# Expert weights in 8 KB and 4 KB rows: gate and up weights with channel d at partition d // 8, down weights as two full-width blocks

## What is computed

```python
mod = c_act @ ada_w[l] + ada_b[l]
shift1, scale1, gate1, shift2, scale2, gate2 = jnp.split(mod, 6, axis=-1)
h = rms_norm(x, norm1_g[l]) * (1.0 + scale1) + shift1
x = x + gate1 * hybrid_mixer(h, ...)
h = rms_norm(x, norm2_g[l]) * (1.0 + scale2) + shift2
# grouped_moe: a router picks one of 4 groups of 4 experts for each token, and 2 experts in it
for e in range(16):
    hid = silu(t @ w_gate[e]) * (t @ w_up[e])        # t: 256 x 1024, w_gate, w_up: 1024 x 512
    out = out + combine[:, e:e + 1] * (hid @ w_down[e])   # w_down: 512 x 1024
x = x + gate2 * out
```

## Time and profile before

| | us |
|---|---|
| median of 3 runs | 1594.67 |
| lowest and highest | 1593.94, 1601.77 |
| the profiled execution | 1598.07 |
| its span, first to last instruction | 1596.3 |

### The profile page before, as it was taken

The page is one execution under the profiler, slowest core; times in us unless marked ns, Lnnn a source line. Parts: engine busy times, 40 slices in busy tenths (PEclk is TensorE's granted clock), DMA queues, the critical chain, the costliest instruction groups (busy, mean ns, idle before and its releaser), DMA issues. The chain is left out here.

```text
span 1596.3 us, 18784 instructions
## 1 busy us (share of the span) xinstructions
PE 1418.2 (89%) x7456; PEld 1138.3 (71%) x7456; DVE 1168.3 (73%) x1292; ACT 792.8 (50%) x738; POOL 227.8 (14%) x188
## 2 busy tenths in 40 slices
PE   1887889998689999999988868899985999999998
PEld 1766687786589977766558657777865999776654
DVE  5599358884568878789866963788646665788886
ACT  2465434443353446567655553433434433566674
POOL 2445231110001200000016633111000000000000
PEclk9898999998889999999989989999987999999999
DMA  9634147982078879899965431588704655799994
GB/s 323 201 106 132 53 145 262 309 290 77 17 248 290 306 267 314 299 320 370 340 176 183 131 96 64 193 281 299 255 0 158 213 208 186 266 340 346 355 356 180
DMA packets 175864, 357.44 MB, mean 224 GB/s; under 512 B 13436, under 2 KB 19808, under 8 KB 174752
## 3 DMA queue, kind: packets, MB, share of 16 engines
q1 hardware_dynamic: 163040, 310.99, 56.7%
q0 software_dynamic: 12736, 45.25, 8.1%
HBM read 355.16 MB, written 1.05 MB: 223 GB/s over the span
## 5 line engine op out<-in xcount | busy, mean ns | idle before, releaser
L1517 DVE TENSOR_TENSOR w_low<-ring,w_high_qk_score 128x2048 fp32r<-128x2048 f32 x84 | 192.4, 2291 | 100.7 <-ACT w_high_qk_score L1075 65.5
L604 PE MATMUL bank<-h_high,w_low 128*128 128x256 f32 x864 | 246.2, 285 | 0.0
L1517 DVE TENSOR_TENSOR w_low<-ring,w_high_xbc_sc 128x2048 fp32r<-128x2048 f32 x82 | 187.9, 2291 | 74.2 <-ACT w_high_xbc_sc L1075 44.4
L1517 DVE TENSOR_TENSOR w_low<-ring,w_high_zu 128x2048 fp32r<-128x2048 f32 x82 | 187.7, 2288 | 19.6 <-ACT w_high_zu L1075 10.2
L603 PE MATMUL bank<-w_low,h_high 128*128 128x512 f32 (+2 forms) x480 | 187.2, 390 | 0.0
L1075 ACT ACTIVATE w_high_xbc_sc<-ring 128x2048 fp32r<-128x2048 f32 x64 | 122.8, 1918 | 97.0 <-PE bank L604 97.0
L604 PEld LDWEIGHTS bank<-h_high,w_low 128*128 128x128 f32 x864 | 166.5, 193 | 0.0
L1075 ACT ACTIVATE w_high_qk_score<-ring 128x2048 fp32r<-128x2048 f32 x64 | 122.8, 1918 | 81.2 <-PE bank L604 81.0
L1075 ACT ACTIVATE w_high_zu<-ring 128x2048 fp32r<-128x2048 f32 x64 | 122.4, 1913 | 71.4 <-PE bank L604 71.4
L603 PE MATMUL bank<-w_low,rows_high 128*128 128x512 f32 (+2 forms) x384 | 150.9, 393 | 0.0
L540 POOL TENSOR_TENSOR w_low<-ring,early_high 128x2048 fp32r<-128x2048 f32 (+1 forms) x28 | 125.5, 4494 | 132.5 <-ACT early_high L1083 132.5
(11 more groups left out here) (442 smaller groups left out, 3577.9 us busy)
## 6 DMA issues: line engine op xcount, KB each, us to landing
ring<-in_w_in SPq DMA_DIRECT2D x64, 1024.0 KB, 5.0
ring<-in_exp_w_gate SPq DMA_DIRECT2D x64, 1024.0 KB, 5.5
ring<-in_exp_w_up SPq DMA_DIRECT2D x64, 1024.0 KB, 6.0
ring<-in_exp_w_down SPq DMA_DIRECT2D x64, 1024.0 KB, 5.2
ada_buf<-in_ada_w POOLq DMA_DIRECT2D x40, 512.0 KB, 6.3
PT<-in_ada_w POOLq DMA_DIRECT2D x40, 512.0 KB, 6.8
ring<-in_w_branch SPq DMA_DIRECT2D x12, 1024.0 KB, 5.2
ring<-in_w_out SPq DMA_DIRECT2D x8, 1024.0 KB, 6.6
```

Of the source, the lines that this page charges most:

```text
L604: return mm(out_, ll, rh, start=False, stop=stop, skip_group_check=True)
L1517: V.tensor_tensor(w_low[:, slot, :, cols], ring[:, slot, :, cols], high[:, :, cols], ALU.subtract).then_inc(w_split, 1)
```

## The change

- `w_gate` and `w_up`: channel d is at partition d // 8, block d % 8. A unit (half of the blocks) is then 8 KB in a row for each partition. So that h agrees, the second norm writes `merged` sorted by d % 8 (ACT and DVE read `x_sb` with a step of 8 values), `router_w` is loaded in the same order, the matmuls of `mod67` and `mod89` take every eighth column of `ada_acc`, and `norm2_g` and the two biases of the second norm come in three DMAs of their own on POOL's queue into `cols2` and no longer through `prow` (now 74 rows).
- `w_down`: a unit holds two of the four blocks of 128 FF channels with all 1024 columns, 4 KB in a row. `dense_down` and `rows_down` write both banks from each unit; the last half-sum of a layer waits for the new semaphore `tail_half`.
- `dense_project` and `turn_hidden` are written otherwise but issue the same instructions.

```diff
-for _name, _n in (("norm1", KD), ("norm2", KD), ("adab", 6 * KD), ("scw", SC_K * CT), ("gvg", CT),
+for _name, _n in (("norm1", KD), ("adab", 2 * KD), ("scw", SC_K * CT), ("gvg", CT),
                   ("mcw", M_K * 6), ("mcb", 6), ("mng", CT)):
...
+        cols2 = turns[:, :, :, :].rearrange("p a t f -> p (a t f)")[:, 0:3 * KD].rearrange("p (i k) -> p i k", i=3)
...
-        columns_in = sem("columns_in")
+        columns_in, tail_half = sem("columns_in"), sem("tail_half")
...
-            rows = (("norm1", norm1_g[layer]), ("norm2", norm2_g[layer]), ("adab", ada_b[layer]),
+            rows = (("norm1", norm1_g[layer]), ("adab", ada_b[layer, 0:2 * D_MODEL]),
...
-            wg_v = exp_w_gate.rearrange("l e (k p) n -> (l e) p k n", p=P)
-            wu_v = exp_w_up.rearrange("l e (k p) n -> (l e) p k n", p=P)
+            wg_v = exp_w_gate.rearrange("l e (p k) n -> (l e) p k n", k=KD)
+            wu_v = exp_w_up.rearrange("l e (p k) n -> (l e) p k n", k=KD)
...
-            sp.dma_start(rw[:, :, :], router_w.rearrange("(k p) e -> p k e", p=P)).then_inc(rw_in, 16)
+            sp.dma_start(rw[:, :, :], router_w.rearrange("(p k) e -> p k e", k=KD)).then_inc(rw_in, 16)
...
 
-                def half(n, src):
+                def half(n, src, dst=None):
                     sp.wait_ge(units_read, l * UNITS_L + MOE0 + n + 1)
-                    load(n % RING, src)
+                    load(n % RING, src, dst)
+
+                def down_half(n, expert, j):
+                    half(n, wd_v[expert, :, 2 * j:2 * j + 2, :],
+                         ring[:, n % RING, :, :].rearrange("p (k c) n -> p k (c n)", c=2))
 
...
                     last = this
                 for j in range(2):
-                    half(down_unit(NE - 1) + j, wd_v[last, :, :, j * W:j * W + W])
+                    down_half(down_unit(NE - 1) + j, last, j)
 
             for t in range(TT):
                 sp.wait_ge(x_tile, DEPTH * 4 - 1 + t)
...
+                for i, v in enumerate((ada_b[l, 3 * D_MODEL:4 * D_MODEL], ada_b[l, 4 * D_MODEL:5 * D_MODEL], norm2_g[l])):
+                    pool.dma_start(cols2[:, i, :], v.rearrange("(p k) -> p k", k=KD)).then_inc(gateb_in, 16)
...
                     b = begin("v", name)
-                    for i in range(2):
-                        pe.wait_ge(acc_ready, l * GATE_CHUNKS + n + i + 2)
-                        chunk_columns(b, 4 * i, ada_acc[:, (n + i) % 2, :]).then_inc(acc_used, 1)
+                    assert n % 2 == 0
+                    whole = ada_acc[:, :, :].rearrange("p i n -> p (i n)")
+                    pe.wait_ge(acc_ready, l * GATE_CHUNKS + n + 1 + 2)
+                    for k in range(KD):
+                        last = mm(b[:, k:k + 1], whole[:, k::KD], ones[:, 0:1], start=True, stop=True)
+                        if k >= KD - 2:
+                            last.then_inc(acc_used, 1)
 
...
+                def down_parts(n):
+
+                    return [part.rearrange("p (k c) n -> p k (c n)", c=2) for part in parts(MOE0 + n, n % RING)]
...
                     for j in range(2):
-                        n = down_unit(e) + j
-                        w = parts(MOE0 + n, n % RING)
+                        w = down_parts(down_unit(e) + j)
                         for t in range(TT):
-                            for k in range(CT):
-                                last = exact_mm(bank[:, 4 + 2 * t + j, :],
-                                                [part[:, k, t * P:t * P + P] for part in (hid_high, hid_low)],
-                                                [part[:, k, :] for part in w], k == 0, k == CT - 1)
+                            for c in range(2):
+                                for k in range(2):
+                                    kk = 2 * j + k
+                                    last = exact_mm(bank[:, 4 + 2 * t + c, :],
+                                                    [part[:, kk, t * P:t * P + P] for part in (hid_high, hid_low)],
+                                                    [part[:, k, c * W:c * W + W] for part in w], kk == 0, kk == CT - 1)
                         last.then_inc(units_read, 1)
...
                     for j in range(2):
-                        u = down_unit(e) + j
-                        w = parts(MOE0 + u, u % RING)
-                        for k in range(CT):
-                            last = exact_mm(bank[0:n, 4 + j, :], (hidT_high[:, k, 0:n], hidT_low[:, k, 0:n]),
-                                            [part[:, k, :] for part in w], e % EPG == 0 and k == 0,
-                                            e % EPG == EPG - 1 and k == CT - 1)
+                        w = down_parts(down_unit(e) + j)
+                        for c in range(2):
+                            for k in range(2):
+                                kk = 2 * j + k
+                                last = exact_mm(bank[0:n, 4 + c, :], (hidT_high[:, kk, 0:n], hidT_low[:, kk, 0:n]),
+                                                [part[:, k, c * W:c * W + W] for part in w], e % EPG == 0 and kk == 0,
+                                                e % EPG == EPG - 1 and kk == CT - 1)
+                            if e == NE - 1 and j == 1 and c == 0:
+                                last.then_inc(tail_half, 1)
                         last.then_inc(units_read, 1)
...
+                def sorted_in(t, k0, k1):
+
+                    return x_sb[:, t, :].rearrange("p (q k) -> p k q", k=KD)[:, k0:k1, :]
...
                         if t == norm % 2:
                             act.wait_ge(rstd_ready, done + 1)
-                            A(merged[:, 0, :], x_sb[:, 0, :], ACT.Copy, scale=st[:, 2, 2:3]).then_inc(xn_ready, 1)
+                            if norm == 1:
+                                A(merged[:, 0, :], x_sb[:, 0, :], ACT.Copy, scale=st[:, 2, 2:3]).then_inc(xn_ready, 1)
+                            else:
+                                A(merged[:, 0, :].rearrange("p (k q) -> p k q", k=KD), sorted_in(0, 0, KD), ACT.Copy,
+                                  scale=st[:, 2, 2:3]).then_inc(xn_ready, 1)
                     if norm == 2:
                         act.wait_ge(rstd_ready, done + 2)
-                        A(merged[:, 1, W:], x_sb[:, 1, W:], ACT.Copy, scale=st[:, 2, 3:4]).then_inc(xn_ready, 1)
+                        A(merged[:, 1, W:].rearrange("p (k q) -> p k q", k=HK), sorted_in(1, HK, KD), ACT.Copy,
+                          scale=st[:, 2, 3:4]).then_inc(xn_ready, 1)
...
-                    a0 = (0 if norm == 1 else 3) * KD
-                    step(V.tensor_tensor(modc[:, norm - 1, 1, :], mod_sum[:, norm - 1, 0:KD], col("adab", a0, KD),
-                                         ALU.add))
-                    step(V.tensor_tensor(modc[:, norm - 1, 0, :], mod_sum[:, norm - 1, KD:], col("adab", a0 + KD, KD),
-                                         ALU.add))
+                    shift_b, scale_b, g = ((col("adab", 0, KD), col("adab", KD, KD), col("norm1", 0, KD)) if norm == 1
+                                           else [cols2[:, i, :] for i in range(3)])
+                    step(V.tensor_tensor(modc[:, norm - 1, 1, :], mod_sum[:, norm - 1, 0:KD], shift_b, ALU.add))
+                    step(V.tensor_tensor(modc[:, norm - 1, 0, :], mod_sum[:, norm - 1, KD:], scale_b, ALU.add))
                     settle()
                     V.scalar_tensor_tensor(out=modc[:, norm - 1, 0, :], in0=modc[:, norm - 1, 0, :], scalar=1.0,
-                                           in1=col(f"norm{norm}", 0, KD), op0=ALU.add, op1=ALU.mult
-                                           ).then_inc(modc_ready, 1)
+                                           in1=g, op0=ALU.add, op1=ALU.mult).then_inc(modc_ready, 1)
...
-                dve.wait_ge(gateb_in, (l + 1) * 32)
+                dve.wait_ge(gateb_in, (l + 1) * (5 * 16))
...
-                V.tensor_scalar(merged[:, 1, 0:W], x_sb[:, 1, 0:W], st[:, 2, 3:4], None, ALU.mult).then_inc(xn_ready, 1)
+                V.tensor_scalar(merged[:, 1, 0:W].rearrange("p (k q) -> p k q", k=HK),
+                                x_sb[:, 1, :].rearrange("p (q k) -> p k q", k=KD)[:, 0:HK, :], st[:, 2, 3:4], None,
+                                ALU.mult).then_inc(xn_ready, 1)
...
                 for j in range(2):
-                    dve.wait_ge(units_read, l * UNITS_L + MOE0 + down_unit(NE - 1) + j + 1 + RING)
+                    if j == 0:
+                        dve.wait_ge(tail_half, l + 1)
+                    else:
+                        dve.wait_ge(units_read, l * UNITS_L + MOE0 + down_unit(NE - 1) + 2 + RING)
                     gate_sum(3, j * W, j * W + W)
```

More of the change, by code:

```diff
@@ L948, in dense_project @@
                         w = parts(MOE0 + n + h, (n + h) % RING)
-                        chan_project(bank[:, b0:b0 + 2, :], w, h, 0, CT, h_moe).then_inc(units_read, 1)
+                        for m in range(CT):
+                            for k in range(HK):
```

(6 more changed lines are left out.)

10 lines of the change are left out of this document (6 added, 4 removed).

## The result

| | before | after |
|---|---|---|
| median, us | 1596.91 (4 runs) | 1616.43 (4 runs) |
| lowest and highest, us | 1593.94, 1601.77 | 1610.92, 1617.94 |
| the profiled execution, us | 1598.07 | 1610.92 |
| its span, us | 1596.3 | 1609.2 |
| mean granted clock of PE | 0.951 | 0.947 |

The ratio after to before is 1.0118, 95% interval [1.0095, 1.014]. The forecast was no change: 1594.2 us, with a range of 1590 to 1602 us, against a median that was then 1594.67 us over three runs. The two profiled executions differ by 12.85 us in time and 12.9 us in span; that difference is what the traces can explain. Two executions of the sets further down, the profiled one of c2 (2067.68 us, granted clock 0.652) and one of c4 (3110.69 us), stand far from all others of their kernels and are left out of every ratio, and c2's trace is not used.

What follows compares the result with a forecast made beforehand. PE was taken to bound the kernel, with transfers never waited for. The terms, 0 - 0.5 + 0 + 0 + 0 = -0.5 us, took the median of 1594.67 us to 1594.2 us, range 1590 to 1602 us.

Steps and rivals of the forecast that it cites:

- Expert loads: Gate, up and down loads in longer rows: a megabyte in 2.55 instead of 2.93 us, hidden behind PE, 0 us.
- `ada_w` loads: Conditioning weight loads on POOL's queue in experts 1 and 3: shorter PE waits, at most 1.4 us gained, taken as -0.5 us.
- mod67 and mod89: PE's column sums with stepped weight loads: bounds no cost or doubled time, +1.9 us for each of four jobs; taken as 0.
- rival A: Reads with a step of 32 bytes cost double at L566 and norm 2: 7.4 + 1.9 = 9.3 us slower; chance 0.08.
- Second norm: Stepped `x_sb` reads on ACT and DVE: bounds no cost or 0.94 us a layer, 1.9 us in all; taken as 0.
- Small loads: Three more 4 KB DMAs on POOL, shorter `prow`, router weights in longer rows: covered by 17 us, 0 us.
- Order of the down units and the tail: PSUM order of the down units: last half-sum complete six matmuls before the end, not twelve; cover 0.5 us, 0 us.
- B: Rival: transfers slow PE's stream by writing the memory it reads; 29 us faster in the row experts, 1565.7 us; chance 0.05.
- C: Rival: rows stay cut into 2 KB pieces or longer ones are no faster; 1594.7 us; chance 0.12.
- D: Rival: POOL's queue is crowded out by SP's 8 KB packets; +2.4 to +4.8 us, 1597.1 to 1599.5 us; chance 0.10.

Runs made afterwards that it cites:

- c2: The kernel before with only the weight loads of mod67 and mod89 read at a step of 8 values: 1613.47 us, ratio 1.0081.
- c4: a4 again, the changed kernel with contiguous reads for mod67, mod89 and the second norm: 1600.44 us, ratio 1.0008 to the kernel before.
- b1: The kernel before with only the down units in 4 KB rows, their bank order and `tail_half`: 1601.62 us, ratio 1.0019.
- b2: The kernel before with only the gate and up units in 8 KB rows: 1599.25 us, ratio 1.0021.
- a4: The changed kernel with contiguous reads for mod67, mod89 and the second norm: 1601.59 us, ratio 1.0033 to the kernel before.
- d1: The kernel before with each group of column sums for mod67 and mod89 issued twice, all contiguous: 1611.47 us, ratio 1.0085.
- c3: The kernel before with only the second norm's copies on ACT and DVE reading `x_sb` at a step of 8 values: 1599.43 us, ratio 0.9991.
- d2: c2 again, the kernel before with only the stepped weight loads of mod67 and mod89: 1614.20 us, ratio 1.0102.

## Why the prediction was wrong

**What bounds the kernel: right.** PE paces the experts, and no rounding waits for a transfer. The waits of ACT in after, whole run, stand where those of the earlier trace rows stand:

```profile
ACT w_high_xbc_sc L1103 <- PE bank L611: 96.1, 62, 6.4
ACT w_high_qk_score L1103 <- PE bank L611: 80.9, 32, 7.5
```

**Expert loads, 0: right; their size was not.** I worked out 2.55 for 2.93 us a megabyte. In the last row experts the DMA share goes from 0.97 at 342 GB/s to 0.93 at 343, so a full share moves 369 for 353 GB/s, 4.6% more where I had a tenth or more. The price of the first 30 us of the launch does not hold in the experts. Nothing hung on it: b1, b2, a4 and c4 show no gain, and no loss that can be told from the spread of before itself.

**`ada_w` loads, -0.5 us: not shown.** Of PE's waits of the earlier trace rows, the one of 0.80 us is gone in after (its matmul at 576.97 has no idle time before it), and the one of 0.60 us is 0.94 (1295.35). A third, which the prediction did not show, is 1.87 us in both (586.24 in before, 593.07 in after). The waits are thus shorter by some 0.5 us, as forecast, but the time does not show it. The lag of after falls by 5.3 us between 500 and 1110 us. By 580 us it has fallen by 2.2, and in d1, which has the old rows, by 1.2. The other 3.1 us go with the clock: from 660 to 900 us its mean is 0.94 in before and 0.96 in after and in d1, whose lag falls there too.

**mod67 and mod89, 0: the step that failed.** The upper bound stood in the text: double the time, +1.9 us for each of four. It is what happened: 3.74 for 1.84 us. I took the lower end with the words "the nearest row is the contiguous one, of the same size and type". Size and type were not what the change alters; the step was, and no row spoke on that. A missing row is no evidence for the lower end. And had the group cost nothing but its own doubled time, the sum would still have come out too low: 7.4 of the 12.8 us.

**The term that no part of the sum had** is PE's clock, put at nothing without a reason. Behind the longer group eight matmuls follow each other every 0.42 us for 0.23: (332.34 - 328.96) - 8 x 0.23 = 1.5 us. With 1.90 for the group this gives 3.4 us for a lag of 3.47 at mod67. At mod89 before has a slow stretch of its own, and there it comes out at 2.9 us. In all 12.8 us, where rival A had 7.4. The trace of before could have told me. Its mean granted clock is 0.951, and its own mod89 group is followed by a fall (0.79 from 362 to 370 us, shown above): a reason to ask what a longer group would do to the clock.

**Second norm, 0: wrong in size, nearly right in effect.** The copies cost 1.00, 0.50 and 0.19 us more; the bounds had 0.86 and 0.43, and 0.20 for DVE hidden behind ACT. That DVE would stay within ACT's time held: 0.68 against 1.22 us. I hid 0.35 us of ACT's first copy behind its wait for `x_sb`, which is gone from the rows of after. From the first copy's start to the transposes it is 4.65 us for 3.61, 1.04 us more (the bounds had 0.94); the clock in the transposes costs 1.71 us (3.68 - 1.97), more than the copies do. In after the two layers lose 2.5 us each and get half of it back soon; alone, in c3, the change of the second norm costs nothing that can be measured.

**Small loads, 0: right.** POOL issues the three new DMAs at once behind the two old ones and idles for 15 us before the next, as before:

```profile
1004.91 1.07 POOL L553 DMA_DIRECT2D turns<-in_ada_b  x2
1005.97 0.54 POOL L553 DMA_DIRECT2D turns<-in_norm_g  x1
1021.50 0.71 POOL L502 DMA_DIRECT2D ada_buf<-in_ada_w  x1 [15.00 <-DVE oT_gv L1905]
```

**Order of the down units and the tail, 0: right.** The first half's gating starts at 1600.15 us, 1.2 us ahead of the send-back, takes 0.69 and leaves the 0.5 us of cover that I had worked out:

```profile
1600.15 0.69 DVE L2056 TENSOR_TENSOR scratch<-bank,gate_bc 66x512 f32<-66x512 f32 x1 [4.49 <-PE bank L611]
...
1601.35 3.17 PE L1032 MATMUL bank<-scratch,back 66*128 66x512 f32 x7
```

**The rivals.** A named the place, the stepped read and the price of the group itself, but not the clock, and had a chance of 0.08 with the argument that "the rows know no such cost". B fell: matmuls stay 0.23 us apart beside 8 KB rows as beside 2 KB rows. C fell in its first half, as the queue has the packets; of its second half, that longer rows are no faster, little fell, as a full share moves 4.6% more. D fell: the median landing of an `ada_buf` piece is 5.9 us, for 6.3 in the kernel before.

**What stays open.** The timed difference is 1616.43 - 1596.91 = 19.5 us, the traces' 12.9. The profiled execution of after was the fastest of its four, that of before 1.2 us above its median. The stepped loads of mod67 and mod89 alone were 1.0081 and 1.0102, 13 to 16 us; between that and 1.0118 or 1.0130 lie up to some 8 us, which the single parts do not show and whose intervals overlap. They may be the second norm together with the shifted clock, the new rows, or spread; the runs do not tell. No version with the new rows beat the kernel before.

## What to carry to other kernels

Where a change alters how an operand is read, the nearest row is one that reads in that way, not one of the same size; without such a row, price the operation at the upper bound if it lies on the bounding engine's path, or measure it by itself first. A layout that makes long rows in a transfer moves the sorting to somebody: find out who reads at a step, and whether the transfer was waited for at all. And behind a group of one-column matmuls look at the granted clock: making the group longer by 1.9 us cost another 1.5 us here in the work that follows.

## What the runs showed that was not expected

- PE's loads of 128 x 128 fp32 weights: 192 ns contiguous, 198 at a step of 2 values, 262 at 3, 330 at 4, 317 at 6, 335 at 8. ACT's copy of 1024 values: 1.15, 1.22 (2), 2.12 (4), 2.15 us (8).
- DVE at a step of 8: a weighed sum of 512 values 1.24 for 0.75 us, a scaling 0.68 for 0.49. POOL's scaling of 1024 values: 3.82 us, with DVE's sum beside it at 2.02 for 0.69.
- Doubling a contiguous group of column sums costs as much as reading it at a step: +13.5 us of lag (d1) and +12.9 (d2).
- Launches of one kernel differ by over 15 us (1593.16 to 1608.70), and in a launch 3 us of that can be there by 42 us.
